# Norm weights of the last block's queries and keys moved into rotation tables and an eviction scale

## The reference, cut to what matters

```python
def rms_norm(x, g):
    y = xf * lax.rsqrt(jnp.mean(xf * xf, axis=-1, keepdims=True) + EPS) * g
def apply_partial_rotary(t, cos, sin):           # half = 8
    t1, t2, rest = t[..., :half], t[..., half:2 * half], t[..., 2 * half:]
    return concatenate([t1 * c - t2 * s, t2 * c + t1 * s, rest])
def dsw_mixer(h, cos, sin, w_in, q_g, k_g):
    qkv = proj[..., :3 * N_GROUPS * INNER].reshape(B, S, 3, N_GROUPS, N_HEADS, HEAD_DIM)
    q = apply_partial_rotary(rms_norm(qkv[:, :, 0], q_g[:, None, :]), cos, sin)
    k = apply_partial_rotary(rms_norm(qkv[:, :, 1], k_g[:, None, :]), cos, sin)
    # per group: masked softmax(q k^T / 8) v; groups weighted by their log-sum-exp
    return o.reshape(B, S, INNER), gate
```

## Time and profile before

| | |
|---|---|
| median of 3 runs | 2324.68 us (2324.07 to 2329.39) |
| profiled execution | 2333.41 us, span 2331.7 us |
| TensorE busy | 2257.4 us, 97% of the span |
| VectorE busy | 967.4 us, 41% |
| ScalarE busy | 470.8 us, 20% |
| mean granted TensorE clock | 0.988 |

### The profile page before, as it was taken

One profiled execution on the slowest core, in us unless ns is written; L12 is line 12 of the kernel. 1 busy time (PEld: TensorE's weight loads), 2 busy tenths in 40 slices (PEclk: granted clock), 3 DMA queues, 4 the chain that ended last, 5 costly groups with the idle time before them and its releaser, 6 DMA issues.

```text
span 2331.7 us, 48633 instructions
## 1 busy us (share of the span) xinstructions
PE 2257.4 (97%) x21524; PEld 1679.6 (72%) x21524; DVE 967.4 (41%) x1984; ACT 470.8 (20%) x864; POOL 27.0 (1%) x66
## 2 busy tenths in 40 slices
PE   8999999999999999989999999999999999999998
PEld 6888767777688877677877877778778864444444
DVE  3675653655434662332121121121123444676663
ACT  2342311000125331110000000000013331232333
POOL 2000000000000000000000000000000000000000
PEclk9999999999999999999999999999999999999999
DMA  9553255677433433549999999999973323433220
GB/s 374 191 217 135 91 218 197 262 275 308 183 127 127 145 109 127 210 179 399 405 403 400 398 393 407 397 403 403 399 298 109 109 80 137 148 122 132 102 93 19
DMA packets 75527, 537.97 MB, mean 231 GB/s; under 512 B 8552, under 2 KB 8560, under 8 KB 11440
## 3 DMA queue, kind: packets, MB, share of 16 engines
q1 hardware_dynamic: 72864, 526.14, 58.3%
q0 software_dynamic: 1360, 4.85, 0.6%
q10 hardware_dynamic: 1088, 3.81, 0.4%
HBM read 529.90 MB, written 4.85 MB: 229 GB/s over the span
## 4 chain that ended last, share of the span: by engine, by line
PE 91%; DVE 5%; ACT 2%; issue 1%; DMA 0%; DVEq 0%; ACTq 0%; SPq 0%
PE ps L937 20%; PE ps L467 13%; PE ps L478 11%; PE ps L1085 7%; PE ps L511 7%; PE ps L961 7%; PE ps L969 4%; PE ps L780 4%; PE ps L891 3%; PE ps L805 2%; PE ps L555 2%; PE ps L1188 2%; PE ps L1128 1%; PE ps L1319 1%; PE ps L1102 1%
## 5 line engine op out<-in xcount | busy, mean ns | idle before, releaser
L937 PEld LDWEIGHTS ps<-hT,ring 128*64 128x64 f32 x11264 | 476.1, 138 | 46.2 <-issue 41.7
L937 PE MATMUL ps<-hT,ring 128*64 128x96 f32 x11264 | 486.6, 248 | 7.5 <-DVEq L2651 4.2
L1967 DVE TENSOR_TENSOR RA<-ps,RA 128x192 f32<-128x192 f32 (+1 forms) x108 | 45.3, 420 | 665.1 <-PE ps L937 554.1
L467 PE MATMUL ps<-ring,hT 128*128 128x256 f32 x1408 | 310.7, 380 | 0.0
L1548 ACT ACTIVATE RA<-ps 128x192 f32<-128x192 f32 (+2 forms) x159 | 70.0, 440 | 1125.7 <-PE ps L937 588.4
L467 PEld LDWEIGHTS ps<-ring,hT 128*128 128x128 f32 x1408 | 265.4, 190 | 37.9 <-issue 2.5
L478 PE MATMUL ps<-hT,ring 128*128 128x256 f32 (+1 forms) x1280 | 269.0, 370 | 0.1
L478 PEld LDWEIGHTS ps<-hT,ring 128*128 128x128 f32 x1280 | 232.0, 190 | 33.1 <-issue 3.1
L511 PE MATMUL ps<-ring,hT 128*128 128x256 f32 x768 | 176.2, 384 | 2.0 <-DVE hT L1967 1.7
L961 PE MATMUL ps<-ring,RA 128*64 128x512 f32 x704 | 168.0, 594 | 0.3 <-issue 0.3
L511 PEld LDWEIGHTS ps<-ring,hT 128*128 128x128 f32 x768 | 145.6, 193 | 23.7 <-issue 2.4
(11 more groups left out here) (324 smaller groups left out, 2089.6 us busy)
## 6 DMA issues: line engine op xcount, KB each, us to landing
ring<-stream SPq DMA_DIRECT2D x497, 1024.0 KB, 7.5
slots_scratch<-YT ACTq DMA_DIRECT2D x7, 384.0 KB, 8.5
x_rows<-x SPq DMA_DIRECT2D x2, 512.0 KB, 11.8
gates_row<-bgate SPq DMA_DIRECT2D x1, 1024.0 KB, 17.0
QT<-bgate SPq DMA_DIRECT2D x1, 1024.0 KB, 19.0
rows_scratch<-RB ACTq DMA_DIRECT2D x2, 512.0 KB, 4.4
out<-x_rows SPq DMA_DIRECT2D x2, 512.0 KB, 2.6
rowt<-rows SPq DMA_DIRECT2D x1, 460.0 KB, 13.7
```

Source lines behind the costliest of these rows:

```text
L467: m = pe.matmul(ps[:, b, t * UC:(t + 1) * UC], lhs[:, k, t * P:(t + 1) * P], ring[:, s, k * UC:(k + 1) * UC], start=k == 0, stop=k == KC - 1)
L937: m = pe.matmul(ps[64 * j:64 * (j + 1), b, c * CAP:(c + 1) * CAP], ring[:, s, k * UC + c * P + 64 * j:k * UC + c * P + 64 * (j + 1)], hT[: ...
L1967: link(v.tensor_tensor(out, a, b, op), c)
```

## The change

`scaled` no longer multiplies the row by the weights. For the 16 rotated features the weights are multiplied into tables: four tables per token tile (cosine and sine, each with the weights of the first and of the second half of the pair), of 6 x 8 numbers, are made by eight small VectorE instructions at the start of the `fox` stage and stand in the `lam` region of `rowt`. The rotation's four multiplications read these tables. For the other 48 features the weight becomes a scale per partition at the eviction in `turned`: a new constant `dswc` has six columns, one for each group of queries and of keys, with 1 at the rotated features. A group of four transposed blocks spans two such columns, so each eviction of 128x512 becomes two of 128x256, with the function Identity and a scale in place of Copy.

```diff
--- before.py
+++ after.py
@@ -96,7 +96,7 @@
 for _name, _n in [("c", KC), ("bmod", 2 * 48), ("n1", 2 * KC), ("n2", 2 * KC), ("router", KC * NE),
                   ("convw", 2 * 32), ("convb", 2 * 8), ("aq", 2), ("ak", 2), ("subln", 2), ("gnorm", 2),
                   ("cnorm", 2), ("lb", 2 * HEADS), ("wif", 2 * KC * 8), ("ng", 2 * KC), ("foxwf", KC * 16),
-                  ("foxq", 1), ("foxk", 1), ("ib", 2), ("fb", 2)]:
+                  ("foxq", 1), ("foxk", 1), ("dswc", 2 * DG), ("ib", 2), ("fb", 2)]:
     COLS[_name] = (sum(n for _, n in COLS.values()), _n)
 N_COLS = sum(n for _, n in COLS.values())
 
@@ -278,6 +278,9 @@
         def row(name):
             o, n = ROWS[name]
             return rowt[:, o:o + n]
+
+        COS_A, SIN_A, COS_B, SIN_B = (
+            row("lam")[:, 96 * i:96 * (i + 1)].rearrange("p (t g j) -> p t g j", t=T, g=6) for i in range(4))
 
         landed = [sem(f"landed{s}") for s in range(RING)]
         unit_done = sem("unit_done")
@@ -1915,7 +1918,12 @@
 
                 def turned(qd, t):
                     for g in range(3):
-                        blocks_out(("dswT", qd, t, g), D_QT[qd % 2][:, 4 * g:4 * g + 4, t * P:(t + 1) * P])
+                        b = bank_of(act, ("dswT", qd, t, g))
+                        for i in range(2):
+                            n = 4 * g + 2 * i
+                            link(fn(D_QT[qd % 2][:, n:n + 2, t * P:(t + 1) * P],
+                                    ps[:, b, 2 * i * P:2 * (i + 1) * P].rearrange("p (n s) -> p n s", n=2),
+                                    ACT.Identity, scale=col("dswc", 2 * g + i)), *([took] if i else []))
 
                 for t in (1, 0):
                     for i in range(2):
@@ -2818,6 +2826,11 @@
                     norm_rows(0)
                     norm_out("ndsw", 0, col("ng", KC, KC))
 
+                weights = row("dswg").rearrange("p (g d) -> p g d", g=6)
+                for t in range(T):
+                    for table, angle, at in ((COS_A, cosr, 0), (SIN_A, sinr, 0), (COS_B, cosr, ROT), (SIN_B, sinr, ROT)):
+                        tt(table[:, t], weights[:, :, at:at + ROT], angle[:, t, :].unsqueeze(1).broadcast_to([P, 6, ROT]),
+                           ALU.mult)
                 link(v.memset(F_QA[:, :, 0:4, 65:66], 1.0))
                 link(v.memset(F_QA[:, :, 4:8, 64:65], 1.0))
                 squares(0)
@@ -2853,15 +2866,10 @@
                     r = rows[:, t, 0:1536].rearrange("p (n d) -> p n d", n=24)
                     tt(r, r, meansq[:, 24 * t:24 * t + 24].unsqueeze(2).broadcast_to([P, 24, 64]), ALU.mult)
                     rg = rows[:, t, 0:1536].rearrange("p (g h d) -> p g h d", g=6, h=4)
-                    wg = row("dswg").rearrange("p (g d) -> p g d", g=6).unsqueeze(2).broadcast_to([P, 6, 4, 64])
-                    tt(rg, rg, wg, ALU.mult)
-
-                    a, b_ = r[:, :, 0:ROT], r[:, :, ROT:2 * ROT]
-                    cc = cosr[:, t, :].unsqueeze(1).broadcast_to([P, 24, ROT])
-                    ss = sinr[:, t, :].unsqueeze(1).broadcast_to([P, 24, ROT])
-                    w = [D_SQ[:, i * 192:(i + 1) * 192].rearrange("p (n j) -> p n j", n=24) for i in range(4)]
-                    for o, i0, i1 in ((w[0], a, cc), (w[1], b_, ss), (w[2], b_, cc), (w[3], a, ss)):
-                        tt(o, i0, i1, ALU.mult)
+                    a, b_ = rg[:, :, :, 0:ROT], rg[:, :, :, ROT:2 * ROT]
+                    w = [D_SQ[:, i * 192:(i + 1) * 192].rearrange("p (g h j) -> p g h j", g=6, h=4) for i in range(4)]
+                    for o, i0, table in ((w[0], a, COS_A), (w[1], b_, SIN_B), (w[2], b_, COS_B), (w[3], a, SIN_A)):
+                        tt(o, i0, table[:, t].unsqueeze(2).broadcast_to([P, 6, 4, ROT]), ALU.mult)
                     tt(a, w[0], w[1], ALU.subtract)
                     tt(b_, w[2], w[3], ALU.add, c=gave_pe if t else step)
 
@@ -2996,6 +3004,9 @@
     put("foxwf", unit_of(inp["fox_w_in_2"][0], 4 * D, 16))
     put("foxq", inp["fox_q_norm_2"][0][:, None])
     put("foxk", inp["fox_k_norm_2"][0][:, None])
+    dsw_g = np.concatenate([inp["dsw_q_norm_2"].reshape(DG, 64), inp["dsw_k_norm_2"].reshape(DG, 64)])
+    dsw_g = np.where(np.arange(64) < 2 * ROT, 1, dsw_g)
+    put("dswc", np.concatenate([dsw_g, dsw_g], axis=1).T)
     lam = np.stack([inp[f"a_lambda_{n}"] for n in ("q1", "k1", "q2", "k2")], axis=1).reshape(-1)
     rows = np.concatenate([lam, inp["moe_router_b"].reshape(-1), inp["fox_b_f_2"].reshape(-1),
                            inp["dsw_q_norm_2"].reshape(-1), inp["dsw_k_norm_2"].reshape(-1)])[None, :]
```

## The result

The changed kernel takes 2320.57 us in the median of 8 runs (2315.38 to 2321.44), the kernel before 2328.26 (2324.07 to 2331.57) beside it. The ratio is 0.9969 with a 95% interval of 0.9956 to 0.9982: a gain of 0.31%, 7.2 us, where 9.7 were predicted.

What follows compares the result with a forecast made beforehand. TensorE, busy 97% of the span, was taken as the bound. Three later turns gaining 11.64 us, less 1.98 lost in the first quad's turn, gave -9.66: median 2324.68 to 2315.0 us, range 2311.5 to 2321.

Steps and rivals of the forecast that it cites:

- VectorE's chain: Each later turn: two 1.79 us multiplications leave VectorE, so TensorE's pause before the transposes falls from 4.13 to 0.55 us.
- The clock behind the turn's pause: Behind the shorter pause of later turns clock stays up; stretch through wide block takes 5.87 us for 7.17, gain 1.30.
- The evictions: ScalarE's two halves at 0.475 us each make 1.01 us per block, 0.38 more; a turn's second half loses 1.00 us.
- No table load came with the new function: Rival: a 1.28 us load before the first eviction of four turns adds 5.1 us, giving 2320.1; chance 0.04.
- The sum per turn: Each of the three later turns takes 10.36 us against 14.24, gaining 3.88 us, 11.64 in three.
- The lead: First quad's turn in the last block: six evictions take 6.03 us instead of 4.05, a loss of 1.98 us.
- the clock falls in new places: Rival: longer evictions' pauses drop the clock in the turns, about 1.30 us each; all four +5.2, 2320.2 us; chance 0.26.
- In the lead the same 3.58 us are worth nothing: First quad's turn: VectorE's 3.58 us earlier end gains nothing, because the first eviction waits for the table load.
- At 1.0 us per activation: Case in the rival that ScalarE becomes the bound, chance 0.03: block eviction time 2.06 us gives 2333.6 us.
- the free operand: Lower bound on eviction cost: the scale adds nothing, 0.83 us per block; sum -12.9 us, giving 2311.8.

Runs made afterwards that it cites:

- h3: Changed kernel with VectorE's weight multiplication kept for all quads, tables without weights and scales of one, leaving only the new evictions; 2334.39 us, ratio 1.0036.
- f1: Kernel before the change, with seven filler matmuls in the 4.1 us pause in front of each later turn; 2321.34 us, ratio 0.9980.
- h2: Changed kernel with both halves of each eviction as plain copies, leaving out the weights of the 48 unrotated features; 2313.28 us, ratio 0.9942.
- f2: Changed kernel with five filler matmuls before the third transpose group of the first quad's turn and two before its scores; 2318.16 us, ratio 0.9968.
- e1: Changed kernel with the first quad's turn done as before: VectorE's multiplication, plain 128x512 copies, old rotation; 2313.84 us, ratio 0.9938.
- f3: Changed kernel whose first quad keeps VectorE's multiplication, with evictions in the new halves at a scale of one; 2318.34 us, ratio 0.9967.
- e3: Changed kernel with plain 128x512 copies at the turns' evictions, leaving out the weights of the 48 unrotated features; 2307.87 us, ratio 0.9913.
- e4: Kernel before the change, with 14 filler matmuls in the 4.1 us pause in front of each later turn; 2327.31 us, ratio 1.0000.
- g1: Changed kernel with first quad's turn as before; later turns apply combined weights to queries only, copy keys plainly and turn key groups first; 2312.99 us, ratio 0.9946.
- g2: g1 with the exponential's table loaded before the last two wide copies of the first quad's projection instead of after them; 2309.55 us, ratio 0.9928.
- h1: The changed kernel run and profiled once more, with nothing altered; 2315.79 us, ratio 0.9965 to the kernel before.
- e2: Changed kernel with filler matmuls in the first quad's turn: ten before the third transpose group, one before each later group, three before scores; 2317.30 us, ratio 0.9952.

## Where the prediction was right, and where it failed

- **VectorE's chain: right.** Two instructions of 1.79 us left each turn, and the pause went from 4.13 to 0.53 us (0.55 predicted). h3, with the instruction back and all else changed, has 4.11.
- **The clock behind the turn's pause: right, as a whole.** It stays at 1.00, and the stretch to the end of the wide half is 5.69 us, for 5.87 predicted and 7.17 before: 1.48 gained, for 1.30. f1 shows the clock's own share, 1.86 us in this turn; the 1.48 are what is left of it after the first eviction's 0.38.
- **The evictions: right.** A half takes 0.473 us on average (0.475 predicted). The second half of a turn is 3.95 us for 3.94. By the Trainium skill (ScalarE: Activation LUTs, What ACT_TABLE_LOAD costs) each per-partition operand adds about 93 ns; the trace agrees with it: 473 less the 384 of a plain copy is 89, and h2's halves as plain copies take 384. No table load came with the new function: there are 86 before and after.
- **The sum per turn: right.** 4.0 us, for 3.88.
- **The lead: the step that failed.** The prediction wrote "a loss of 1.98 us", from the evictions alone; the lead's clock stands in its sum at nothing. The late evictions do cost that (2.0 us in f2, with the clock up). But the lead's clock falls, which adds 2.4 us in the changed kernel's first profile and 1.7 in its second. e1 takes the lead out of the change and finds 4.34 us.
- **The rival "the clock falls in new places": true in one place,** the one it named, with a pause of 2.40 us for its 2.2 (the first transposes start not 0.62 but 0.78 us sooner, right behind the projection). It priced a fall at 1.30 us; measured ones cost between some 0.35 us (f3) and 2.4, by how long the clock is down and by what TensorE has to do while the clock is down: little where it waits anyhow, most where the scores and 16 long matmuls follow. The prediction treated forecast and rival as alternatives; the place where a pause was known to double should have stood in the sum itself.
- **"In the lead the same 3.58 us are worth nothing" was wrong too.** Earlier transposes only lengthen the pause behind them, since the table load fixes when the first eviction starts, and behind the longer pause the clock fell: e3's lead lost 2.3 us, with the evictions of before.
- **Two slips in its numbers change nothing.** At 1.0 us per activation its own sum gives 2333.9 and not 2333.6, and the range's lower end, said to be that of the free operand, is 2311.5 where the sum has 2311.8.

The gain by steps is then 3.60 (VectorE) + 1.86 (clock) - 0.38 - 1.01 (evictions) = 4.07 in the second quad's turn, and 12.06 - 4.46 = 7.60 in all.

**Still open** is what decides whether, and where, the clock falls. Lead pauses of 1.16 to 1.18 us (before, e1, e4, f1, g1) and of 0.31 (g2) left it at 1.00. With each of those of 1.55 (f3, h3), 2.02 (e3), 2.22 (h2) and 2.40 (changed, h1) it fell, but in h1 only 6 us after the pause. So the longer pause goes with the fall in all of six leads and the shorter with none in six; a pause between 1.18 and 1.55 us was not tried. In later turns of the six executions with scaled halves and a short first pause (changed, e1, e2, f2, f3, h1) it fell in 3 of 18, though from the wide half on the pauses of a turn were the same to 0.01 us in all of them. One profiled execution of each does not give a rate, and f2's misses may be no more than this scatter.

## What to carry to other kernels

An edit that ends a wait of the bound engine has to be followed to every place where the same code runs: here the change was worth 4 us in each of three turns and cost 4.4 in the lead, where another engine held the next step. Work that makes a producer earlier lengthens the pause behind it if what comes next doesn't move; where that pause falls between short matmuls, price the clock in the sum, by the work that stands behind it. If a fixed thing, such as a table load, sets that pause, move it first.

## What the runs showed of the hardware

- The granted clock fell to 0.50 in a turn's second half with TensorE never idle there for more than 0.89 us at a time: pauses of 0.89, 0.45 and 0.40 us between groups of transposes of 0.5 to 1.0 us (f2, e2), though the same rows in other executions kept it at 1.00.
- One program had the fall within its lead's pause of 2.40 us, 3 us behind the projection's end, or 9.4 us behind it, and 0.8 us of difference in the last block (changed, h1).
- Two kernels with the same work and the same pause of 1.55 us in the lead lost 0.35 and 2.0 us there by the clock's fall (f3, h3), which came 3.5 and 5.8 us behind the projection's end.
- Of a pause of 4.13 us the clock's part is 1.86 us on top: filler that ends before the wait is over brings it back (f1), filler that outlasts it by 1.8 us spends it (e4).
